# Two transformer blocks on one core: index dots among the projections, key selection in front of attention, and leaner recurrences

## The reference

```python
# first block ("a" in the kernel), per layer
h = rmsnorm(x); z = h @ w_in                       # q k v | rq rk rv rg | ga gb
ya = sliding_window_sink_attention(rope(q), rope(k), v, sinks) @ w_a
r  = chunkwise_retention(rot(rq), rot(rk), rv)      # 4 heads, 128 x 256
r  = r * rsqrt(mean(r*r)+eps) * silu(rg);  yb = r @ w_b
x  = x + (sigmoid(ga)*ya + sigmoid(gb)*yb) @ w_out
x  = x + square(relu(rmsnorm(x) @ w_up)) @ w_down

# second block ("b"), per layer; 8 heads of 64, 8 index heads of 64
proj = x @ w_in    # aq ak av | iq ik iw | gq gk gv g_lr g_r | gate_a gate_b
I[t,s] = sum_h iw[t,h] * relu(iq[t,h] . ik[s]) / 8      # index scores
keys of t = the 128 admissible s with the largest I[t,s]   # chunk-causal, chunks of 64
ya = softmax over those keys(aq . ak / 8) @ av @ p_attn
S_c = exp(total_c) * S_(c-1) + k_dec^T v;  o = q S_c       # GLA, 4 heads, 8 chunks of 64
o  = (o - mean(o)) * rsqrt(var(o)+eps) * g * silu(g_r);  yb = o @ p_gla
x  = layer_norm(a*x + (sigmoid(gate_a)*ya + sigmoid(gate_b)*yb) @ w_out + b)
x  = layer_norm(a*x + conv_ffn(x))
```

## Time and profile before

| | us |
|---|---|
| runs (median of 3; lowest, highest) | 3798.99; 3798.47, 3800.3 |
| the profiled execution, its own time | 3792.64 |
| its span, first to last instruction | 3790.8 |
| TensorE busy (matmuls) | 3531.3 (93%) |
| VectorE, ScalarE, GpSimd busy | 1740.2, 1439.5, 1268.3 |
| mean granted TensorE clock | 0.969 |

### The profile page before, as it was taken

The page is one execution under the profiler, slowest core; times in us unless marked ns, Lnnn a source line. Parts: engine busy times, 40 slices in busy tenths (PEclk is TensorE's granted clock), DMA queues, the critical chain, the costliest instruction groups (busy, mean ns, idle before and its releaser), DMA issues.

```text
span 3790.8 us, 44190 instructions
## 1 busy us (share of the span) xinstructions
PE 3531.3 (93%) x16402; PEld 2845.0 (75%) x16402; DVE 1740.2 (46%) x2391; ACT 1439.5 (38%) x1852; POOL 1268.3 (33%) x278
## 2 busy tenths in 40 slices
PE   7999999999899999999779998999897899989997
PEld 5788778877688788878558776787685677768885
DVE  5624342336524643347851344434578613344445
ACT  3644232223734232233643334333335343343333
POOL 3233434433233434433112232444241122324432
PEclk9999999999999999999899999999999999999999
DMA  3121222221122222222111121222221111212221
GB/s 134 56 75 71 92 86 100 89 107 73 56 78 89 89 89 98 94 87 89 45 45 66 58 81 66 89 100 89 78 79 56 45 56 56 78 67 100 89 100 55
DMA packets 43809, 298.47 MB, mean 79 GB/s; under 512 B 4816, under 2 KB 5456, under 8 KB 8592
## 3 DMA queue, kind: packets, MB, share of 16 engines
q1 hardware_dynamic: 41696, 291.52, 20.8%
q10 hardware_dynamic: 1968, 4.94, 0.4%
HBM read 294.34 MB, written 2.10 MB: 78 GB/s over the span
## 4 chain that ended last, share of the span: by engine, by line
issue 72%; POOL 15%; PE 10%; DVE 1%; ACT 1%; POOLq 0%; DVEq 0%; ACTq 0%
POOL w_lo L306 15%; PE ps L404 3%; PE ps L406 3%; PE ps L405 3%; PE ps L486 0%; ACT x L1376 0%; DVE arena L1585 0%; ACT arena L1074 0%; POOLq L303 0%; DVE x L1620 0%; DVE arena L1608 0%; DVE tmp L1413 0%; ACT y_hi L1093 0%; DVE x L1827 0%; ACT x_hi L908 0%
## 5 line engine op out<-in xcount | busy, mean ns | idle before, releaser
L306 POOL TENSOR_TENSOR w_lo<-w_raw,w_hi 128x2048 fp32r<-128x2048 f32 x274 | 1268.1, 4629 | 2481.6 <-ACT w_hi L899 2481.6
L404 PE MATMUL ps<-x_hi,w_hi 128*128 128x512 f32 x2752 | 1103.6, 401 | 41.2 <-DVE x_lo L1398 25.9
L405 PE MATMUL ps<-x_lo,w_hi 128*128 128x512 f32 x2752 | 1084.8, 394 | 0.0
L406 PE MATMUL ps<-x_hi,w_lo 128*128 128x512 f32 x2752 | 1084.1, 394 | 0.0
L899 ACT ACTIVATE w_hi<-w_raw 128x2048 fp32r<-128x2048 f32 x274 | 522.2, 1906 | 507.8 <-PE ps L406 507.8
L404 PEld LDWEIGHTS ps<-x_hi,w_hi 128*128 128x128 f32 x2752 | 526.5, 191 | 162.9 <-DVE x_lo L1398 23.6
L406 PEld LDWEIGHTS ps<-x_hi,w_lo 128*128 128x128 f32 x2752 | 524.9, 191 | 112.6
L405 PEld LDWEIGHTS ps<-x_lo,w_hi 128*128 128x128 f32 x2752 | 526.1, 191 | 109.0 <-issue 2.9
L404 PE MATMUL ps<-y_hi,w_hi 128*128 128x512 f32 x1248 | 493.0, 395 | 25.2 <-DVE x L1620 13.0
L405 PE MATMUL ps<-y_lo,w_hi 128*128 128x512 f32 x1248 | 489.6, 392 | 0.0
L406 PE MATMUL ps<-y_hi,w_lo 128*128 128x512 f32 x1248 | 489.0, 392 | 0.0
(11 more groups left out here) (181 smaller groups left out, 3370.4 us busy)
## 6 DMA issues: line engine op xcount, KB each, us to landing
w_raw<-stream SPq DMA_DIRECT2D x274, 1024.0 KB, 4.8
x<-x_t SPq DMA_DIRECT2D x4, 512.0 KB, 5.6
rotary<-rot ACTq DMA_DIRECT2D x4, 512.0 KB, 3.6
y_t<-x SPq DMA_DIRECT2D x8, 256.0 KB, 2.1
ct<-consts ACTq DMA_DIRECT2D x2, 770.0 KB, 4.3
arena<-pos ACTq DMA_DIRECT2D x2, 256.0 KB, 2.4
vec<-vectors ACTq DMA_DIRECT2D x4, 116.0 KB, 2.0
ct<-consts ACTq DMA_DIRECT2D x1, 128.0 KB, 3.4
```

Source lines behind the costliest of these rows:

```text
L306: nc.gpsimd.tensor_tensor(WL[:, s, :], RAW[:, s, :], WH[:, s, :].bitcast(F32), ALU.subtract)\
L404: pe.matmul(ps, wh, xh, start=(k == 0), stop=False)
L405: pe.matmul(ps, wh, xl, start=False, stop=False)
L406: return pe.matmul(ps, wl, xh, start=False, stop=last)
```

## The change

1. The weight stream of the second block is put in the order index q, index k/misc, q, k; `tiles_b` gives each panel's two tiles. VectorE ropes tiles 8 to 12 first.
2. The 12 dots no longer stand behind all projection tiles: `dots_behind(j)` lists the dots that follow q or k tile j on TensorE, their reads on ScalarE, and their weighting on VectorE behind the rope of tile j. The rope's scratch and block 3's score tile move to other buffers.
3. All value tiles and the first four gate tiles come in front of attention. VectorE does 40 of the 48 selection rounds in front of its first softmax step, and one round a pair from pair 1 to 8. Attention draws one dense tile at every second pair (`every` = 2), 8 in all.
4. GLA: value columns are centred when they are read (`value_mean`, and the read adds the negative mean as a bias), and `mean`/`centre` go. The two squares of a head are added on VectorE, so `variance` is one column sum; the same in retention. The state updates use three PSUM banks in turn (`kv_bank`), the wait between the two updates of a pair goes, and updates c+2 and c+3 stand behind output c. The next head's value tiles come ahead of this head's gate tiles.

```diff
-        out += _cols(aq) + _cols(ak) + _cols(iq) + [_panel(misc)] + _cols(av) + _cols(ga)
+        out += _cols(iq) + [_panel(misc)] + _cols(aq) + _cols(ak) + _cols(av) + _cols(ga)
...
+        def tiles_b(i):
+            return (8, 9, 10, 11, 12, 13, 0, 1, 2, 3, 4, 5, 6, 7)[2 * i:2 * i + 2]
+        def dots_behind(j):
+            return ((0, 1), (2,), (3, 4), (5,), (6, 7), (8,), (9, 10), (11,))[j]
+        def kv_bank(h, c):
+            return PS[:, (4, 5, 2)[(8 * h + c) % 3], 0:256]
...   TensorE: projections and dots
-                for i in range(12):
+                def dots(i):
...
+                for i in range(3, 7):
+                    work = gemm_tiles(w["iq"] + i, KD, 2, XH, XL, h_ready, lambda m: (t, l, "q", tiles_b(i)[m]))
+                    for j in tiles_b(i):
+                        run(work)
+                        for u in dots_behind(j):
+                            dots(u)
+                    run(work)
+                for _ in tok_pair(w["v"], "av", h_ready, t, l):
+                    pass
+                for p in range(2):
+                    gemm(w["ga"] + p, KD, 2, XH, XL, h_ready, lambda m: (t, l, "ga", 2 * p + m))
                 def fillers():
-                    for p in range(4):
+                    for p in range(2, 4):
...
-                attention(pairs_b(l), l, t, fillers())
+                attention(pairs_b(l), l, t, fillers(), 2)
...   TensorE: GLA
                     for h in range(GLA_HEADS):
-                        yield from gemm_tiles(w["gv"] + 2 * h + 1, KD, 2, XH, XL, h_ready, lambda m: (t, l, "gr", h, m))
                         if h + 1 < GLA_HEADS:
-                            yield from tok_tiles(w["gv"] + 2 * h + 2, h_ready, lambda m: (t, l, "gv", h + 1, m))
+                            yield from tok_tiles(w["gv"] + 2 * h + 1, h_ready, lambda m: (t, l, "gv", h + 1, m))
+                        yield from gemm_tiles(w["gv"] + min(2 * h + 2, 7), KD, 2, XH, XL, h_ready, lambda m: (t, l, "gr", h, m))
...
-                        if c % 2:
-                            T.after()
-                        else:
-                            T.after((t, l, "state", h, c - 3) if c >= 4 else ((t, l, "state", h - 1, c + 5) if h else None),
+                        if c % 2 == 0:
+                            T.after((t, l, "state", h, c - 2) if c else ((t, l, "state", h - 1, 6) if h else bank_reader[2]),
...   ScalarE: value reads with the mean as bias
+                        A.after((t, l, "gv_mean", h, m), (t, l, "g_out", h - 2, 7) if h >= 2 else None)
+                        for c in range(2):
+                            e, mean = slice(256 * c, 256 * c + 256), 4 * (h % 2) + 2 * m + c
+                            A.done(act.activation(AR[:, 14 + 2 * (h % 2) + m, e], bank_of(t, l, "gv", h, m)[:, e],
+                                                  ACT.Identity, bias=ST[:, mean:mean + 1]), "read", t, l, "gv", h, m)
...   VectorE: ropes, weighting, selection
+                for j in range(8, 13):
+                    rope_b(j)
...
+                for j in range(8):
+                    rope_b(j)
+                    for u in dots_behind(j):
+                        weigh(u)
...
-                attention(pairs_b(l), l, t, top_k(), TOPK // 8 // 4)
+                selection = top_k()
+                run(selection, 2 * (TOPK // 8) + TOPK // 16)
+                attention(pairs_b(l), l, t, selection, 1)
...   VectorE: GLA (retention has the same addition, "r_sq_sum")
+                def value_mean(h, m):
+                    mean = ST[:, 4 * (h % 2) + 2 * m:4 * (h % 2) + 2 * m + 2]
...
+                    V.done(dve.tensor_reduce(mean, bank_of(t, l, "gv", h, m).rearrange("p (c e) -> p c e", c=2), AX, ALU.add))
...
                     if h:
-                        centre(h - 1)
+                        V.after((t, l, "o_sq", h - 1, 0), (t, l, "o_sq", h - 1, 1))
+                        V.done(dve.tensor_tensor(TMP[:, 0, :], TMP[:, 0, :], TMP[:, 1, :], ALU.add), t, l, "o_sq_sum", h - 1)
                     for c in range(4):
                         if h < GLA_HEADS:
                             state(h, c)
+                    if h + 1 < GLA_HEADS:
+                        value_mean(h + 1, 0)
```

More of the change, by code:

```diff
@@ L354, in pairs_b @@
                                 mask=mask_b(b), weight=-NEG, sink=None,
-                                ready=[("b", l, "mask", b)] + [("read", "b", l, "av", p, m) for p in range(2) for m in range(2)],
+                                ready=[("b", l, "roped", 7)] + [("read", "b", l, "av", p, m) for p in range(2) for m in range(2)],
                                 o=AR[:, 8 + j, b * P:(b + 1) * P]))
@@ L516, in inverse_deviation, with attention @@
                 keep_clock(bank, 2)
-            def attention(pairs, l, t, fillers):
+            def attention(pairs, l, t, fillers, every=1):
                 ring[0] = 2
@@ L1269, in tok_reads, with gate_a_reads @@
                             yield
-                fillers = tok_reads(w["v"], "av")
-                run(fillers, 2)
-                for i in range(12):
-                    nk = (i // 4 + 2) * P
-                    A.after((t, l, "dots", i), (t, l, "acc", 2 * (i - 2) + 1) if i >= 2 else None)
-                    A.done(act.activation(probs(i, nk), PS[:, 4 + 2 * (i % 2):6 + 2 * (i % 2), 0:nk], ACT.Relu, scale=0.125),
-                           t, l, "dots_read", i)
-                    if i in (3, 7):
-                        run(fillers)
-                def filler_reads():
-                    for p in range(4):
-                        hi(w["ga"] + p + 1)
-                        for m in range(2):
-                            read((t, l, "ga", 2 * p + m), G[:, 2 * p + m, :], ACT.Sigmoid)
-                            yield
+                for _ in tok_reads(w["v"], "av"):
+                    pass
+                def gate_a_reads(p):
+                    hi(w["ga"] + p + 1)
+                    for m in range(2):
+                        read((t, l, "ga", 2 * p + m), G[:, 2 * p + m, :], ACT.Sigmoid)
+                        yield
+                for p in range(2):
+                    for _ in gate_a_reads(p):
+                        pass
+                def filler_reads():
+                    for p in range(2, 4):
+                        yield from gate_a_reads(p)
                     for p in range(2):
@@ L1371, in _ @@
                     if which == "ln1" or l + 1 < DEPTH:
-                        hi(w["ff"] + 1 if which == "ln1" else at_b(l + 1)["q"] + 1)
+                        hi(w["ff"] + 1 if which == "ln1" else at_b(l + 1)["iq"] + 1)
                     for k in range(KD):
@@ L1669, in _ @@
                 for h in range(RET_HEADS + 1):
+                    if h:
+                        V.after((t, l, "r_sq", h - 1, 0), (t, l, "r_sq", h - 1, 1))
+                        V.done(dve.tensor_tensor(AR[:, 2, :], AR[:, 2, :], AR[:, 3, :], ALU.add), t, l, "r_sq_sum", h - 1)
                     if h < RET_HEADS:
@@ L1709, in _, with rope_b @@
                 V.after("vec2" if l == 0 else "vec3")
-                for j in range(13):
-                    rope(AR[:, j, :], SWAP_B, (t, l, "roped", j), [("read", t, l, "q", j), (t, l, "rot_tables")])
+                def rope_b(j):
+                    rope(AR[:, j, :], SWAP_B, (t, l, "roped", j), [("read", t, l, "q", j), (t, l, "rot_tables")],
+                         YSCR[:, KD + 1, :])
+                for j in range(8, 13):
+                    rope_b(j)
                 iw = ST[:, 32:64].rearrange("p (n h) -> p n h", n=NB)
```

111 lines of the change are left out of this document (56 added, 55 removed).

## The result

The changed kernel took 3776.2 us in the median of four runs (3773.3 to 3778.8), the kernel before, beside it, 3798.7 us (3794.8 to 3800.3): a ratio of 0.9943, 95% interval 0.9931 to 0.9955. It is faster by 22.5 us; the forecast was 46 us. The profiled execution of the changed kernel took 3778.8 us (span 3777.0), that of before 3792.6, so the two traces differ by 13.8 us only: that of before lies 6 us under its median, that of after 2.5 over.

The account below looks back on a forecast made before the run. TensorE was taken to bound nearly all of the second block, except the first softmax wait and attention, where VectorE counts. GLA -23.6, retention -7.2 and attention -15.2 sum to -46.0: 3753 us from 3799.0, 8-in-10 range 3730 to 3782.

Parts of the forecast that it names:

- Retention, -7.2: First block: the retention variance loses one column sum for 4 heads and 2 layers, 7.2 us less, at worst 0.
- GLA, -11.8 a layer (-23.6): Gated recurrence, second block: fewer column sums and update waits, less an added stall, save 11.8 us a layer, 23.6 in all.
- Stall 2.6: GLA head start: TensorE waits 2.6 us for state 0 behind VectorE's addition of the last head's squares.
- fell to half after each pause of 3 us or so: Attention before the change: TensorE's granted clock halved after such pauses, making it busy 11 us more than at full clock.
- nothing: Gated recurrence: the value means on VectorE stand beside 5.5 us tiles and were said to cost no time.
- rival 2: Six GLA heads: the new additions of squares are held up, 4.5 us more stall each, +27, 3780 us; chance 0.06.
- Attention's front and attention, -7.6 a layer (-15.2): Second block up to the recurrence: front 24.6 us longer, attention 32.2 shorter, so 7.6 less a layer, 15.2 in all.
- So VectorE ends level, at worst 7 us late. I take level: Attention's front: VectorE's ropes and weightings keep up with TensorE's tiles, so selection starts 4.7 us behind the last dot.
- Attention itself, 112.8: Attention with 8 dense tiles, one behind every second pair, takes 112.8 us a layer, where it took 145.0 with 12.
- Rival 1: Front: VectorE 7 us behind in each layer, clock as poor as now; attention +5 x 2, 3778 us; chance 0.14.
- a pause over 18 us: Before the first attention scores: a TensorE pause this long would show the forecast wrong; about 13 us was expected.
- the weightings can now fill: Front: argument that half of VectorE's busy 70.0 us are hold-ups of tensor_tensor passes, which the dots' weightings could use.

Follow-up runs that it names:

- the recurrence alone: The kernel before with only the gated recurrence's new form added: 3779.1 us, ratio 0.9956.
- the front alone: The kernel before with only the new order of dots, selection and attention in the second block: 3788.5 us, ratio 0.9979.
- the late addition: The changed kernel with VectorE's addition of the previous head's squares put behind the next head's first four states: 3753.4 us, ratio 0.9889.

## Why the prediction was wrong

By its own steps, for both layers together:

- **Retention, -7.2:** -6.8 measured alone. Right.
- **GLA, -11.8 a layer (-23.6):** -16.7 alone, and some 7 to 8 within the whole change. The kinds of work were sized well: without the stall a head takes 30.70 - 0.55 = 30.15 us, where the working had 33.2 - 2.6 = 30.6, and the stall of 2.6 was 2.66. The step that failed is "Stall 2.6": it was priced at its own length. Where the clock falls behind one, which it did behind five of the six in the trace of this part alone, it costs 1.5 us more (seen twice, with most of the wait removed and with the wait filled): 7.4 us, and 23.6 - 7.4 = 16.2 against 16.7 measured. The working had charged attention with a clock that "fell to half after each pause of 3 us or so", but put the clock's cost behind the 2.6 us stall at nothing, without a reason.
- **The later stall:** "nothing" was said of what else VectorE does in the recurrence. The gate's product, held up behind GpSimd with a state in its queue, made a second stall in each layer, in the changed kernel but not with the recurrence alone; moving those states gave 11 us. This accounts for the 9 us by which the parts don't add up, though differences of single timings this small are uncertain by several us. It is a hold-up as rival 2 had it, in another instruction and twice, not six times.
- **Attention's front and attention, -7.6 a layer (-15.2):** -8.0 for both layers, timed alone. "So VectorE ends level, at worst 7 us late. I take level" failed: it was 7.2 us late (11.9 against 4.7), the end given as the worst. The working allowed each panel 0 to 4 us of hold-up and took the balance as even; the trace has one of 4.6 to 5.0 in every one of the four panels, because each gives GpSimd one subtraction and VectorE has almost nothing but two-input passes there. The first transpose came at 156.9 us after the front's first matmul in place of 146.7: 1.8 from the stretch of the dots, 7.2 from this, and 1.2 from the selection and the first softmax (55.9 us where 54.6 was taken). The pause, so counted, was 22.7 in place of 13.4. Over two layers the first transposes are 20.4 us late.
- **Attention itself, 112.8:** 110.1 in the changed kernel, at clock 0.93; it returned 2.7 a layer. With these, -15.2 + 20.4 - 5.4 = -0.2, near the table's -0.5 and -1.1. With the front alone attention took 107.8, at clock 0.96: -15.2 + 20.4 - 10.0 = -4.8, against -8.0 timed. The other 3 us are not accounted for.

Rival 1 named the mechanism and the place of the front's miss, and its sign of being wrong, a pause over 18 us, came. But it gave the front +10 where -8 was measured, since it took a poor clock with it (its terms, 7 us and 11 of clock in place of 7.5, add up to +3 a layer and not to its +5); that its 3778 lies near the 3776 is chance, for the recurrence missed by as much. Its own argument against, "the weightings can now fill" the hold-ups, is what the trace refutes: L1772 with its SBUF operands was itself held up, 4.61 us at 1733.23. Nor were half of VectorE's 70.0 us hold-ups: the six held passes before take 29.0 us in all.

The forecast had cited the Trainium skill ("SBUF — State Buffer", Who interferes with whom) against the additions of squares. The trace agrees with that page, and quartering the subtraction shows what the rule is worth here (35 us); but the rule's weight was in the ropes and weightings of the front, where the working counted it at half its price, and not in the addition of squares: no subtraction ran beside any of the eight (0.69 us each), as rival 2's own argument against had said.

Left open: which passes of the first block the quarters free (its share was not tested apart), what shifts the gate's product by the 0.35 us on which the later stall hangs, and 3 us of the front's gain.

## What to carry to other kernels

A short stall of TensorE in an otherwise dense stretch is not priced at its length: here 2.7 us cost 4.1 where the clock fell behind it, and a stall that can't be removed is worth filling, even with matmuls that nobody reads. When an engine in front of a pause is nearly level with another, count one hold-up for each of the partner's instructions, at the partner's full length (here 4.6 us, four times), and look at whether the partner can be cut into pieces. And look in an engine's queue at what stands in front of the one result that is waited for: two changes of order there gave 31 us, and with a third, of TensorE's tiles, 55, and none of them removed work.

## What the hardware showed that was not expected

- After most stalls of 2.66 us in a dense stretch the granted clock fell to half (9 of 12 in the two traces of the changed kernel), in the case shown 1.9 us after the work had begun again. It stayed there for 3.4 us in five of the nine and for 6.8 in the other four. After a stall of 0.55 us it did not fall at any of the six later heads with the late addition. It did in layer 1 of that trace at the first head, where a wait of 1.86 us stood just ahead of the 0.55.
- GpSimd's subtraction takes 4625 ns for 2048 columns and 4 x 1352 ns for the same in quarters, while the kernel gets faster by 35 us: VectorE gets its turn between two instructions of GpSimd that follow at once.
- A SCALAR_TENSOR_TENSOR with two SBUF inputs was held up (4.61 us at 1733.23) like a TENSOR_TENSOR; the selection's MAX8 and MATCH_REPLACE8 kept to 0.43 and 0.41 us at 256 columns, also in the 16 of 32 rounds that ran beside a subtraction.
- Which of the two starts first decides: a product that began 0.20 us behind a subtraction took 4.91 us, one that began 0.15 us ahead of it took 0.69, and that subtraction 5.00 in place of 4.57.
